# Values of the latent attention kept in memory once as fp32, and split into high and low parts inside the attention

## The reference

```python
cq, ckv, kr, z = split(h @ w_in)                       # 384, 256, 32, 1024 columns
q  = (_rmsnorm(cq, q_norm) @ w_uq)                     # 16 heads x (64 + 32)
kv = (_rmsnorm(ckv, kv_norm) @ w_ukv).reshape(B, S, 16, 64 + 64)
k_nope, v = kv[..., :64], kv[..., 64:]
...
s = (q_nope . k_nope + q_rope . k_rope) * (64 + 32) ** -0.5
pr = softmax(where(causal, s, -1e30))
o = (pr @ v) * silu(z)
```

## Time and profile before

| | |
|---|---|
| median of 3 runs | 3166.45 us (3164.95 to 3171.06) |
| the profiled execution's own time | 3169.97 us |
| its span, first to last instruction | 3168.1 us |
| mean granted clock of PE | 0.970 of full speed |
| busy share of the span: PE, DVE, ACT, POOL | 94%, 60%, 51%, 45% |
| "ukv" jobs, last part of "end0" | about 1638 to 1770 us of the span |
| "mla" phase | 1770 to about 2740 us |

### The profile page before, as it was taken

How to read it: one execution, slowest core, us unless ns; L and a number is a source line. 1 busy time by engine, 2 the same in 40 slices (tenths; PEclk the granted TensorE clock), 3 DMA queues, 4 the chain that set the end, 5 groups by cost and what they waited for, 6 DMA issues and landing times. The chain is left out here.

```text
span 3168.1 us, 41018 instructions
## 1 busy us (share of the span) xinstructions
PE 2963.8 (94%) x13536; PEld 2326.5 (73%) x13536; DVE 1893.9 (60%) x2692; ACT 1629.4 (51%) x2830; POOL 1430.8 (45%) x1158
## 2 busy tenths in 40 slices
PE   7999987888999999999988699999999999899998
PEld 6888875555788788777766377777777777588876
DVE  3544313343378765555653578788787787357875
ACT  3111113557435544444554177777777777644553
POOL 0022103556222540000563088888888888623353
PEclk9999998999999999999998599999999999999999
DMA  5355449875997675554899743443533533399674
GB/s 164 82 126 119 119 136 208 203 193 165 282 293 242 216 240 179 175 168 154 272 375 337 198 98 71 101 99 71 117 83 79 119 71 101 92 305 280 223 235 147
DMA packets 297350, 549.53 MB, mean 173 GB/s; under 512 B 30976, under 2 KB 118656, under 8 KB 289984
## 3 DMA queue, kind: packets, MB, share of 16 engines
q1 hardware_dynamic: 222912, 399.62, 44.9%
q10 hardware_dynamic: 74240, 147.49, 15.4%
HBM read 366.24 MB, written 180.49 MB: 173 GB/s over the span
## 5 line engine op out<-in xcount | busy, mean ns | idle before, releaser
L2475 POOL TENSOR_TENSOR mla_pl<-mla_p,mla_ph 128x512 fp32r<-128x512 f32 (+3 forms) x640 | 707.6, 1121 | 202.8 <-ACT mla_p L2349 194.3
L1479 PE MATMUL end_bank<-end_xh,end_whi 128*128 128x512 f32 x1808 | 717.7, 397 | 45.7 <-DVE end_wlo L1710 17.9
L1480 PE MATMUL end_bank<-end_xl,end_whi 128*128 128x512 f32 x1808 | 708.3, 392 | 0.0
L1481 PE MATMUL end_bank<-end_xh,end_wlo 128*128 128x512 f32 x1808 | 707.6, 391 | 0.0
L1548 ACT CAST end_whi<-early_wraw 128x1024 fp32r<-128x1024 f32 (+1 forms) x228 | 235.0, 1031 | 578.4 <-PE end_bank L1481 527.2
L2348 ACT ACTIVATE mla_ph<-mla_score 128x512 fp32r<-128x512 f32 (+3 forms) x640 | 341.8, 534 | 225.3 <-PE mla_score L2199 217.1
L1710 DVE TENSOR_TENSOR end_wlo<-early_wraw,end_whi 128x1024 fp32r<-128x1024 f32 x188 | 254.1, 1352 | 320.1 <-ACT end_whi L1548 320.1
L1479 PEld LDWEIGHTS end_bank<-end_xh,end_whi 128*128 128x128 f32 x1808 | 342.4, 189 | 133.9 <-DVE end_wlo L1710 25.4
L2376 DVE TENSOR_REDUCE mla_mx<-mla_mx 128x1 f32<-128x512 f32 (+3 forms) x640 | 372.4, 604 | 87.6 <-PE mla_mx L2199 86.9
L2422 DVE TENSOR_TENSOR mla_acc<-mla_acc,mla_p 128x512 f32<-128x512 f32 (+3 forms) x576 | 349.2, 606 | 120.2 <-ACT mla_p L2349 115.7
L1480 PEld LDWEIGHTS end_bank<-end_xl,end_whi 128*128 128x128 f32 x1808 | 342.5, 189 | 72.8 <-issue 2.9
(11 more groups left out here) (234 smaller groups left out, 4992.1 us busy)
## 6 DMA issues: line engine op xcount, KB each, us to landing
early_wraw<-in_pe_gate ACTq DMA_DIRECT2D x64, 512.0 KB, 5.2
early_wraw<-in_w_out ACTq DMA_DIRECT2D x62, 512.0 KB, 7.2
early_wraw<-in_w_in ACTq DMA_DIRECT2D x56, 512.0 KB, 3.8
swa_q<-scratch_q_hi SPq DMA_DIRECT2D x32, 512.0 KB, 10.1
end_factor<-scratch_inv SPq DMA_DIRECT2D x64, 256.0 KB, 9.7
scratch_proj<-end_out_f SPq DMA_DIRECT2D x64, 256.0 KB, 6.6
scratch_sum<-end_out_f SPq DMA_DIRECT2D x64, 256.0 KB, 6.0
end_old<-scratch_proj SPq DMA_DIRECT2D x64, 256.0 KB, 3.6
```

The costliest lines, as they stand in the source:

```text
L1479: nc.tensor.matmul(bank, wh[:, at], xh[:, k0 + k, :], start=(k == 0), stop=False)
L1480: nc.tensor.matmul(bank, wh[:, at], xl[:, k0 + k, :], start=False, stop=False)
L1481: last = nc.tensor.matmul(bank, wl[:, at], xh[:, k0 + k, :], start=False, stop=(k == kc - 1))
L2475: pool.tensor_tensor(p_lo[b][:, off:TC], prob[b][:, off:TC], p_hi[b][:, off:TC].bitcast(F32), ALU.subtract).then_inc(p_lo_ok, 1)
```

## The change

The values are no longer split where they are made. The new name `values_at` is 20. A `v` tile is now copied by DVE alone, as fp32, into a place of the six that the `split` tiles use, and stored with 256 KB. The array in memory has 64 columns for each head in place of 128. ACT has no part in a `v` tile. In the latent attention the loads go to two new tiles `v_raw`, of half the size, with rows of 64 numbers (256 B) in place of 128, and the split is made there for each unit: `values_high` on ACT (a copy of 128x1024 numbers) ahead of the exponentials of step 20 of the unit before, and `values_low` on DVE (a subtraction of 128x1024) ahead of the items of slot 21. For the first unit they stand before `max_row(0)` and after `negate(0)`. PE waits for `values_low` at the first `weigh` of each unit, and SP's load of the values waits for `values_low` of two units before in place of the last `weigh`.

```diff
@@ chain_phase
-        out_tiles = [n for n, x in enumerate(tiles) if x["kind"] not in ("turn", "v")]
+        out_tiles = [n for n, x in enumerate(tiles) if x["kind"] != "turn"]
...
                 elif kind == "v":
-                    sp.dma_start(latent["v"][x["i"], :, 4 * q + x["at"], :], v_tile(n).rearrange(
-                        "p h two d -> p (h two d)")).then_inc(v_stored[values[n] % 3], 16)
+                    sp.dma_start(latent["v"][x["i"], :, 4 * q + x["at"], :], out_f[place[n]][:]
+                                 ).then_inc(stored[place[n]], 16)
...
-                elif x["kind"] == "v":
-                    act.wait_ge(product, n + 1)
-                    wait_v_free(act, n)
-                    act.copy(v_tile(n)[:, :, 0, :].bitcast(F32R), bank.rearrange("p (h d) -> p h d", d=HEAD_DIM)
-                             ).then_inc(hi_ok, 1)
...
                 elif x["kind"] == "v":
-                    dve.wait_ge(hi_ok, highs[n])
-                    vec.tensor_tensor(v_tile(n)[:, :, 1, :].bitcast(F32R), bank.rearrange("p (h d) -> p h d", d=HEAD_DIM),
-                                      v_tile(n)[:, :, 0, :], ALU.subtract).then_inc(dve_out, 1)
+                    dve.wait_ge(product, n + 1)
+                    wait_out_free(dve, n)
+                    vec.tensor_copy(out_f[place[n]][:], bank).then_inc(dve_out, 1)
@@ attention_phase (long is true for "mla")
+            v_raw = [s.sb(f"v_raw{b}", [P, vb, HEAD_DIM]) for b in range(2)]
...
                     if n == cfg["n_load_b"] - 1 and u >= 2:
-                        sp.wait_ge(weighed, ends[u - 2])
+                        if long:
+                            sp.wait_ge(v_lo_ok, u - 1)
...
+                if long and k == 0:
+                    pe.wait_ge(v_lo_ok, u + 1)
...
+            def values_high(u):
+                act.wait_ge(ld_b[u % 2], 16 * cfg["n_load_b"] * (u // 2 + 1))
+                if u >= 2:
+                    act.wait_ge(weighed, ends[u - 2])
+                act.copy(vals[u % 2][:, :, 0:HEAD_DIM], v_raw[u % 2][:]).then_inc(v_hi_ok, 1)
...
+            if long:
+                values_high(0)
             max_row(0)
             for g in range(total + tail):
                 if g < total:
                     u, k, st = flat[g]
+                    if long and k == values_at and u + 1 < units:
+                        values_high(u + 1)
...
+            def values_low(u):
+                dve.wait_ge(v_hi_ok, u + 1)
+                vec.tensor_tensor(vals[u % 2][:, :, HEAD_DIM:P], v_raw[u % 2][:],
+                                  vals[u % 2][:, :, 0:HEAD_DIM].bitcast(F32), ALU.subtract).then_inc(v_lo_ok, 1)
...
             negate(0)
+            if long:
+                values_low(0)
             for g in range(total + tail):
                 if g < total:
                     u, k, st = flat[g]
+                    if long and k == values_at + 1 and u + 1 < units:
+                        values_low(u + 1)
                     for n in at_slot(u, k):
                         item(u + 1, n)
                     add(g)
```

More of the change, by code:

```diff
@@ L1126, in chain_phase @@
         outs, olds, turns = upto("pe"), upto("wo", "pe"), upto("pe", "z")
-        highs, rotated, values = upto("split", "v"), upto("turn", "kr"), upto("v")
+        highs, rotated = upto("split"), upto("turn", "kr")
         def row_of(x):
@@ L1144, in chain_phase @@
         turn_tiles = [n for n, x in enumerate(tiles) if x["kind"] == "turn"]
-        v_tiles = [n for n, x in enumerate(tiles) if x["kind"] == "v"]
         def row_ends(n):
@@ L1231, in chain_phase @@
         turn_stored = [s.sem(f"turn_stored{b}") for b in range(2)]
-        v_stored = [s.sem(f"v_stored{b}") for b in range(3)]
         block = ctx.enter_context(nc.Block())
@@ L1273, in wait_w_lo @@
                 eng.wait_ge(w_lo_p_ok, b - n_dve_blocks + 1)
[L1275 to L1288, removed]
         def wait_old_in(eng, n):
@@ L1452, in _ @@
                     sp.wait_ge(turn_stored[b], 16 * len(turn_tiles))
-                for b in range(3):
-                    sp.wait_ge(v_stored[b], 16 * sum(values[n] % 3 == b for n in v_tiles))
         @block.tensor
@@ L2055, in attention_phase @@
         vals = [s.sb(f"v{b}", [P, vb, P if long else 2 * P], F32R) for b in range(2)]
+        if long:
+            v_raw = [s.sb(f"v_raw{b}", [P, vb, HEAD_DIM]) for b in range(2)]
+            v_hi_ok, v_lo_ok = s.sem("v_hi_ok"), s.sem("v_lo_ok")
         prob = [s.sb(f"p{b}", [P, TC]) for b in range(nbuf)]
@@ L2147, in at_slot @@
             return mine[k] if k < len(mine) and u + 1 < units else []
+        values_at = 20
         tail = store_lag + 1
@@ L2170, in load_low @@
                     sp.wait_ge(scores, ends[u - 2])
-                for n, (dst, src) in enumerate(cfg["load_b"](u, q_tiles[1][u % 2], k_tiles[1][u % 2], vals[u % 2])):
+                v_tile = v_raw[u % 2] if long else vals[u % 2]
+                for n, (dst, src) in enumerate(cfg["load_b"](u, q_tiles[1][u % 2], k_tiles[1][u % 2], v_tile)):
                     if n == cfg["n_load_b"] - 1 and u >= 2:
-                        sp.wait_ge(weighed, ends[u - 2])
+                        if long:
+                            sp.wait_ge(v_lo_ok, u - 1)
+                        else:
+                            sp.wait_ge(weighed, ends[u - 2])
                     sp.dma_start(dst.bitcast(F32), src).then_inc(ld_b[u % 2], 16)
@@ L2590, in load_b @@
         half_heads = HEADS // 2
-        yield vals[:], v[u // half_heads].rearrange("p n (h d) -> h p n d", d=P)[u % half_heads]
+        yield vals[:], v[u // half_heads].rearrange("p n (h d) -> h p n d", d=HEAD_DIM)[u % half_heads]
     def rows_of(x, u, c):
@@ L2684, in build @@
         qn, qr = parts("qn", [HEADS // 2, P, SEQ]), parts("qr", [2, 2, P, SEQ])
-        kr, kn, v1 = parts("kr", [ROPE, SEQ]), parts("kn", [HEADS // 2, P, SEQ]), dram("v1", [2, P, NB, HEADS // 2 * P])
+        kr, kn, v1 = parts("kr", [ROPE, SEQ]), parts("kn", [HEADS // 2, P, SEQ]), dram("v1", [2, P, NB, HEADS // 2 * HEAD_DIM])
         mla = mla_config(qn, qr, kn, kr, v1, z1, o1, den1, loads1, here)
```

## The result

The changed kernel takes 3202.22 us (median of 4 runs, 3199.49 to 3204.01) against 3166.01 in the runs beside it: 1.0109 times as long, 95% interval 1.0096 to 1.0123. It is 36 us slower, where +24.5 was forecast.

What follows compares the result with a forecast made beforehand. PE, busy for 94% of the span, was taken as the bound, held up in the ukv jobs by stores of values. The terms -25 + 37.5 + 12 gave +24.5 us on 3166.45, so 3191 us, range 3166 to 3209.

Steps and rivals of the forecast that it cites:

- Part 1: ukv jobs and the tail behind them: `v` tile stores of half the bytes save 25 us.
- rival 3: ukv jobs: the shared places run short and only 17 us are won; +33 us in all, 3199 us; chance 0.10.
- Part 2, the stall: Latent attention, slot 22: PE waits 2.5 us for late maxima in each of 15 units, +37.5 us.
- POOL in the way: Latent attention, slot 21: `values_low` waits 0.65 us per unit for POOL, counted within the stall.
- Clock: Latent attention, behind the stall: PE drops to half clock in half of the units, 1.6 us each, +12 us.
- Waits moved, rows of 256 B: Latent attention: the new waits of PE, SP and ACT cost nothing; the smaller-row load takes at most 17.8 us.
- The first: Latent attention: the same stall, but the clock stays up; +12.5 us in all, 3179 us; chance 0.27.
- The second: Latent attention: DVE has slack before slot 22, so the stall is small; -8 us in all, 3158 us; chance 0.10.
- The fifth: Latent attention: slow 256 B rows hold ACT before step 20; a 30 us load adds +75 us, 3266 us; chance 0.03.
- The fourth: Latent attention: the clock falls in every unit and POOL always interferes; +43 us in all, 3209 us; chance 0.10.

Runs made afterwards that it cites:

- e6: The changed kernel with three 256 KB places of their own for the `v` tiles instead of the six shared ones: 3219.46 us, 1.0172 of the kernel before.
- e5: The changed kernel with each `v` tile stored twice, so as many bytes are written as before the change: 3219.27 us, 1.0174 of the kernel before.
- e2: The changed kernel with only the subtraction on DVE moved, to slot 36: 3156.10 us, 0.9968 of the kernel before.
- e3: The changed kernel with only the copy on ACT moved, to step 17: 3189.92 us, 1.0074 of the kernel before.
- e7: The changed kernel with the copy on ACT moved to step 18 and the subtraction on DVE to slot 36: 3145.80 us, 0.9934 of the kernel before.
- e1: The changed kernel with the copy on ACT moved to step 37 and the subtraction on DVE to slot 38: 3195.33 us, 1.0089 of the kernel before.
- e4: The changed kernel with the subtraction on DVE made in two halves, at slots 21 and 34: 3192.55 us, 1.0083 of the kernel before.

## Why the prediction was right

- *Part 1, -25 us.* It measured -24 (-26.3 with the drift ahead of it). The size is right, and that is in part luck. I counted bytes at an unchanged rate, and the rate was unchanged (351 against 347 GB/s), but only because more places came with the change: e6 has the same bytes with three places, moved 318 GB/s and gained 13 us. By e5 the bytes are worth 15 us with six places, by e6 13 with three, and the rest, 9 to 12 us, is the places, which the prediction held for a danger (rival 3) where they were nearly half of the gain. That ACT's leaving is worth little by itself agrees with both: the bytes alone (e5 to changed) gave 15, the bytes and ACT's part together (before to e6) 13.
- *Part 2, the stall, +37.5 us.* Spacing 3.77 less 1.55 for the clock leaves 2.2 us per unit, 33 in all, against 2.5 and 37.5 forecast. Its links came out one by one: 0.61 us of delay in `add` (0.66), `values_low` at 1.80 (1.22 + 0.65), the copy at 1.03 (1.04), PE's wait before the items of slot 22 (1.83 and 0.20). e2 isolates ACT's part at 0.6, e3 that of DVE and POOL at 1.7; they add up to the whole within 0.1.
- *POOL in the way.* The 0.6 us are in every unit, and absent only where POOL has no work. By the Trainium skill ("SBUF — State Buffer", section "SBUF: two separate sides") the two shut each other out for a whole instruction; DVE's 1202 against 1804 ns and POOL's 4.74 us for three instructions agree with it.
- *Clock, +12 us.* This term was mis-sized. One drop costs what was forecast (1.55 us against 1.6), but it was to happen in half of the units, a choice between two rows that disagreed, and happened in all 15: 15 x 1.55 = 23 us. These 11 us too little are larger than the whole difference between +24.5 and the +33 of the spans; the stall, 4 us too much, took part of it back. What is left nearly cancels: 1 us in part 1, 1 us in the attention, and in code that the change doesn't touch 2 us more in the end of layer 1 and 2 us less ahead of the ukv jobs.
- *Waits moved, rows of 256 B.* Nothing came of either in time. The load lands in 15.7 us with half the bytes, 17.8 with all, in as many rows. Most of this is not the load's own: in the packet records its first row starts 11.4 us after the issue before and 11.6 after, behind the other loads of the unit. A row of 256 B then took 24 ns of a DMA engine in the mean, one of 512 B 35 ns. So a byte in a row of 256 B does cost more, 1.4 times here; the Trainium skill ("DMA: Bandwidth & Descriptors", section "Specifications") asks for at least 512 B for the full rate, and in its direction the trace agrees. The 25 us that the load had are not used up. ACT was idle before a copy for want of its load only in the first unit, whose cover held.
- *The rivals.* The first (clock stays up) is refuted for the changed kernel, and is what e2 and e7 have. The second asked for slack before slot 22, and there is none. The third's wait is there, but short: DVE's copies waited 12.4 us for stores of keys, and PE 6.2 us for these copies. The fifth did not come. The fourth comes closest, by its clock.

What stays open: why the same 1.22 us of idle time is followed by half clock in one unit of e3 and not in the next, and why e5 moves bytes at 382 GB/s where the kernel before had 346. To the first the clock records add that it is not chance: in e3 the drop begins 1.2, 1.7 and 2.2 us behind the stall in three units in a row, the next unit has none, then it is 1.3, 1.8, 2.3 and none again. What else the place of the stall is measured against, no run here shows. How the gain of the places would look with the 512 KB tiles of before was not tried.

## What to carry to other kernels

Work that is spread over a phase bound by one engine is free only where the engine that gets it has slack up to the next thing that the bound engine waits for. Look at the one step, not at the share of busy time: DVE was idle for a fifth of the unit, and 1.8 us before slot 21's items cost 1.7 us of PE, and the half clock behind it nearly as much again. Put each half of such a pair where its own engine waits (here ACT at step 18, DVE at slot 36), and look one step further for who comes next, as e1 shows. For stores count both the bytes and the places: with few places a smaller tile does not fill the DMAs.

## What the runs showed of the hardware that was not expected

PE idle for 1.22 to 1.83 us in an otherwise full stretch was followed by 3.4 us at half clock (1.2 in place of 2.4 GHz) in most units: 15 of 15 in the changed kernel (1.83 us), 13 of 15 in e4 (1.30), 11 of 15 in e3 (1.22); idle stretches of 0.2 to 0.7 us never were, in e2 and e7. The length alone does not decide: 2.4 us in e1 had it in 12 of 14, and 1.83 us in e6 in 14 of 15, two of them 6.8 us long. Each drop of 3.4 us costs 1.55 to 1.6 us, nearly as much again as the shorter stalls themselves. And a `tensor_tensor` of DVE with both inputs in SBUF took 1.2 us alone and 1.8 us beside POOL's own `tensor_tensor`, the same in every place where it was put (1804, 1808, 1810 and 1777 ns at the median in the changed kernel, e1, e3 and e7).
